# Hybrid decoder step on one core: input projections of both layers by Strassen's seven block products, and four buffers of weight sums in the dense down projection

## What is computed

```python
h = rmsnorm(x, p['norm_mix'][l])                     # (288, 1024)
proj = (h @ p['w_in'][l]).astype(f32)                # its first 3072 columns are retention's q, k, v, g
q, k, v, g = split_cols(p_ret, (512, 512, 1024, 1024))
...
def swiglu(h, w1, w3, w2):                           # layer 0, D_FF = 2816
    return (jax.nn.silu(h @ w1) * (h @ w3)) @ w2
```

## Time and profile before

| what | value |
| --- | --- |
| three runs | 2597.69, 2598.03, 2598.75 us; median 2598.03 |
| the profiled execution | 2598.95 us, of which 2597.1 us are the span from first to last instruction |
| TensorE (PE) busy | 2537.8 us, 98% of the span |
| VectorE (DVE) busy | 984.4 us, 38% |
| ScalarE (ACT) busy | 591.7 us, 23% |
| mean granted TensorE clock | 0.996 |

### The profile page before, as it was taken

How to read it: one execution, slowest core, us unless ns; L and a number is a source line. 1 busy time by engine, 2 the same in 40 slices (tenths; PEclk the granted TensorE clock), 3 DMA queues, 4 the chain that set the end, 5 groups by cost and what they waited for, 6 DMA issues and landing times. The chain is left out here.

```text
span 2597.1 us, 92064 instructions
## 1 busy us (share of the span) xinstructions
PE 2537.8 (98%) x41094; PEld 1990.9 (77%) x41094; DVE 984.4 (38%) x2719; ACT 591.7 (23%) x1773; POOL 0.2 (0%) x4
## 2 busy tenths in 40 slices
PE   8999999999999999999999999999999999999998
PEld 5766666666678999676666666667899999999997
DVE  2022665666515675202267566651311111111111
ACT  2232333333301100123333333330111111111111
POOL 0000000000000000000000000000000000000000
PEclk9999999999999999999999999999999999999999
DMA  6433442222243443333334222234699999999997
GB/s 223 122 121 113 158 153 92 81 77 76 96 143 127 151 155 126 123 114 132 135 127 158 91 84 81 76 104 130 253 371 395 376 368 389 388 370 378 392 370 277
DMA packets 145584, 499.71 MB, mean 192 GB/s; under 512 B 18736, under 2 KB 23472, under 8 KB 142800
## 3 DMA queue, kind: packets, MB, share of 16 engines
q1 hardware_dynamic: 145360, 496.43, 53.6%
HBM read 476.07 MB, written 20.29 MB: 191 GB/s over the span
## 5 line engine op out<-in xcount | busy, mean ns | idle before, releaser
L295 PE MATMUL psum<-hT,ring 128*64 128x288 f32 (+1 forms) x4376 | 540.4, 391 | 1.8 <-DVE hT L2084 1.8
L410 PE MATMUL psum<-work,ring 128*64 128x88 f32 x11264 | 434.7, 239 | 3.5 <-issue 3.5
L410 PEld LDWEIGHTS psum<-work,ring 128*64 128x64 f32 x11264 | 433.2, 136 | 5.9 <-issue 5.7
L295 PEld LDWEIGHTS psum<-hT,ring 128*64 128x64 f32 x4376 | 292.4, 137 | 160.3 <-issue 8.1
L2309 PE MATMUL psum<-work,proj 128*64 128x88 f32 x5632 | 223.7, 239 | 1.0 <-issue 1.0
L2309 PEld LDWEIGHTS psum<-work,proj 128*64 128x64 f32 x5632 | 218.3, 136 | 5.7 <-issue 5.7
L403 PE MATMUL psum<-hT,ring 128*128 128x288 f32 x768 | 187.1, 406 | 0.0
L1461 ACT ACTIVATE work<-psum 128x256 f32<-128x256 f32 (+4 forms) x320 | 104.0, 362 | 349.9 <-PE psum L1374 84.8
L2586 DVE TENSOR_TENSOR work<-psum,work 128x88 f32<-128x88 f32 x176 | 44.2, 251 | 367.6 <-PE psum L410 367.6
L403 PEld LDWEIGHTS psum<-hT,ring 128*128 128x128 f32 x768 | 145.8, 190 | 40.9 <-issue 0.8
L2392 ACT ACTIVATE work<-psum 128x88 f32<-128x88 f32 x176 | 43.1, 245 | 380.5 <-PE psum L410 380.5
(11 more groups left out here) (449 smaller groups left out, 3293.8 us busy)
## 6 DMA issues: line engine op xcount, KB each, us to landing
ring<-w_ff_dram SPq DMA_DIRECT2D x424, 512.0 KB, 6.5
ring<-w_mix_dram SPq DMA_DIRECT2D x256, 512.0 KB, 3.8
proj<-w_ff_dram SPq DMA_DIRECT2D x128, 512.0 KB, 5.4
proj<-w_ff_dram SPq DMA_DIRECT2D x64, 384.0 KB, 5.6
work<-s_gla_dram SPq DMA_DIRECT2D x8, 1024.0 KB, 5.1
gla_s_out<-work SPq DMA_DIRECT2D x8, 1024.0 KB, 4.7
work<-s_ret_dram SPq DMA_DIRECT2D x8, 512.0 KB, 4.7
ret_s_out<-work SPq DMA_DIRECT2D x8, 512.0 KB, 3.1
```

The costliest lines, as they stand in the source:

```text
L295: last = nc.tensor.matmul(out[64 * c:64 * c + 64], weights[:, 64 * c:64 * c + 64], x, start=start, stop=stop)
L410: mm = nc.tensor.matmul(out[64 * c:64 * c + 64], ring[:, s, k, 64 * c:64 * c + 64], rhs[:, k0 + k, :], start=(k0 + k == 0), stop=(k0 + k = ...
```

## The change

It does two things. `project_in` handles its 24 slabs as 12 pairs by the seven block products, with `weight_sums`, `activation_sums`, `combine` and the products moved out of `mix_out` into shared helpers. And the down part of the dense feed-forward uses the same `wsum` memory as four buffers (its sums are at most 128x256), forms sums up to three slabs ahead, waits for them later inside a slab, and puts `combine` and the additions of a group behind the sums of the third slab of the next group.

```diff
+    def seven_products(pe, sig, q, a1, a2, sums, xsums, h, ready=lambda k: None):
+        s1, s2, s3, s4 = sums
+        t1, t2, t3, t4 = (xsums[:, i] for i in range(4))
+        x, y, z = FIRST[q % 2], MIDDLE[q % 2], LAST_TWO[q % 2]   # banks 0,3 / 1,4 / 2,5
+        block_group(x[:, 2 * HALF:3 * HALF], a1[:, 0:4], h[:, 0:4, 0:HALF], ...)
+        block_group(x[:, 0:HALF], a1[:, 4:8], h[:, 4:8, 0:HALF], ...)
+        pe.wait_ge(sig("wsum"), 4 * q + 3)
+        block_group(x[:, HALF:2 * HALF], s2, t2).then_inc(sig("first_ps"), 1)
+        block_group(y[:, 0:HALF], s1, t1)
+        block_group(y[:, HALF:2 * HALF], s3, t3).then_inc(sig("middle_ps"), 1)
+        pe.wait_ge(sig("wsum"), 4 * q + 4)
+        block_group(z[:, 0:HALF], s4, h[:, 4:8, HALF:T])
+        block_group(z[:, HALF:2 * HALF], a2[:, 4:8], t4).then_inc(slab_done, 2)
 # retention, TensorE
-            pe.wait_ge(projected("bank_free"), 3 * RING)
+            pe.wait_ge(projected("evacuated"), 4)
+            pe.wait_ge(projected("taken"), 11)
 # mix_out, TensorE, down part
-                    pe.wait_ge(sig("wsum"), 4 * (FT + n) + 4)
...
+                        if k == 0:
+                            pe.wait_ge(sig("wsum"), 4 * (FT + n) + 3)     # before the third product
...
+                        if k == 0:
+                            pe.wait_ge(sig("wsum"), 4 * (FT + n) + 4)     # before the sixth
 # mix_out, VectorE, down part (sums of slab n in buffer n % 4)
-                dve.wait_ge(slab_done, FF0 + UP_SLABS + (n - 1 if n >= 2 else 2 * n - 2))
+                dve.wait_ge(slab_done, FF0 + UP_SLABS + (n - 3 if n >= 4 else n // 2 * 2 - 2))
...
                     else:
                         down_weight_sums(0)
+                        down_weight_sums(1)
...
-                for n in range(1, DOWN_SLABS + 1):
...
+                for n in range(2, DOWN_SLABS):
+                    down_weight_sums(n)
+                    if n % 6 == 2 and n > 6:
+                        add_pair(n // 6 - 1)          # combine, two add_slab
+                    if n % 6 == 4 and n > 6:
+                        add_squares(n // 6 - 1)
+                add_pair(KT // 2 - 1)
+                add_squares(KT // 2 - 1)
 # project_in, TensorE
-            for n in range(3 * RING):
-                slab_arrived(pe, S_RET, n // RING, n % RING)
-                if n >= 4:
-                    pe.wait_ge(sig("bank_free"), n - 3)
-                slab_products(pe, n % RING, bank[n % 4][:, 0:T], hT)
-                if n == 1:
+            for p in range(PAIRS):                    # 12
+                pair_arrived(pe, p)
+                if p == 1:
+                    pe.wait_ge(sig("z"), 1)
+                if p >= 2:
+                    pe.wait_ge(sig("taken"), p - 1)
+                seven_products(pe, sig, p, ring[...], ring[...], sum_tiles(wsum[:, p % 2], 4, 4), xsum, hT)
+                if p == 0:                            # the four gate products Z, as before
 # project_in, ScalarE
+            def take_first(p):                        # copies one product, 128x144, out of its bank
+            def evacuate(p, func=cp):                 # quad (four quarters, 128x576) -> proj
+                act.wait_ge(sig("taken"), p + 1)
-            evacuate(0)
-            evacuate(1)
+            take_first(0)
             act.wait_ge(sig("z_ps"), 1)
             for h in range(GLA_H):
                 last = ac(z[:, h, :], Z[h][:, 0:T], ...)
             last.then_inc(sig("z"), 1)
+            evacuate(0)
+            take_first(1)
...
 # project_in, VectorE
+            def pair_sums(p):
+                pair_arrived(dve, p)
+                if p >= 2:
+                    dve.wait_ge(slab_done, slabs_before(layer, S_RET) + 2 * p - 2)
+                weight_sums(...)
+            def pair(p):
+                if p >= 2:
+                    dve.wait_ge(sig("evacuated"), p - 1)
+                combine(...)
             # order after the norm: activation_sums, sums 0, mix x2, sums 1, pair 0, sums 2,
             # [wait z, L2753, L2754], pair 1, sums 3, [L2757, L2759], pair 2, sums 4,
             # [scans L2764, in layer 0 the cast L2767], then for p = 3..11: pair p, sums p + 2
```

More of the change, by code:

```diff
@@ L412, in narrow_products, with flat, sum_tiles, block_group @@
         mm.then_inc(slab_done, 1)
+    FIRST, MIDDLE, LAST_TWO = bank[0:6:3], bank[1:6:3], bank[2:6:3]
+    def flat(ap):
+        return ap.rearrange("p n t -> p (n t)")
+    def sum_tiles(region, n, blocks):
+        return (region[:, i, 0:128 * blocks].rearrange("p (k m) -> p k m", m=128) for i in range(n))
+    def block_group(out, weights, x, ready=lambda k: None):
+        for k in range(PAIRS_UP):
+            ready(k)
+            last = in_halves(out, weights[:, k], x[:, k], start=(k == 0), stop=(k == PAIRS_UP - 1))
+        return last
@@ new lines, in combine @@
+    def combine(dve, sig, q, done, c, first):
+        two = lambda b: b[:, 0:2 * HALF].rearrange("p (n t) -> p n t", n=2)
+        dve.wait_ge(sig("first"), q + 1)
+        nc.vector.tensor_tensor(c[:, 0:5:4, :], two(FIRST[q % 2]), rep(first, 1, 2), ALU.add).then_inc(sig("u2"), 1)
+        dve.wait_ge(sig("u2"), q + 1)
+        dve.wait_ge(sig("middle_ps"), q + 1)
+        nc.vector.tensor_tensor(c[:, 5:7, :], two(MIDDLE[q % 2]), rep(c[:, 4, :], 1, 2), ALU.add).then_inc(sig("u34"), 1)
+        dve.wait_ge(sig("u34"), q + 1)
+        dve.wait_ge(slab_done, done)
+        nc.vector.tensor_tensor(c[:, 1:3, :], two(LAST_TWO[q % 2]), c[:, 5:7, :], ALU.add).then_inc(sig("outer"), 1)
+        nc.vector.tensor_tensor(c[:, 3, :], MIDDLE[q % 2][:, 0:HALF], c[:, 6, :], ALU.add).then_inc(sig("taken"), 1)
@@ L1848, in _ @@
         def _(pe):
[L1849 to L1856, removed]
             def logits(k):
@@ L2080, in _, with add_pair, add_squares @@
+            def add_pair(q):
+                c = quad[:, (FT + q) % 2]
+                combine(dve, sig, FT + q, FF0 + UP_SLABS + 6 * q + 6, c, first_product[:, (FT + q) % 2, :])
+                dve.wait_ge(sig("taken"), FT + q + 1)
+                for r in range(2):
+                    add_slab(KT + 2 * q + r, flat(c[:, 2 * r:2 * r + 2, :]))
+            def add_squares(q):
+                for m in range(2 * q, 2 * q + 2):
+                    add_square(KT + m)
             if dense:
@@ L2767, in _ @@
                 nc.vector.tensor_copy(masks[:, :], masks32)
+            for p in range(3, PAIRS):
+                pair(p)
+                if p + 2 < PAIRS:
+                    pair_sums(p + 2)
     for layer in range(DEPTH):
```

168 lines of the change are left out of this document (82 added, 86 removed).

## The result

The changed kernel takes 2579.03 us (median of 4 runs, 2576.24 to 2581.84) against 2598.04 for the kernel before (4 runs, 2597.69 to 2598.75): a ratio of 0.9927, with an interval from 0.9911 to 0.9943. It is faster by 19.0 us, where 26.2 were forecast. Its profiled execution took 2580.26 us, with a span of 2578.4 us and a mean granted clock of 0.995.

The account below looks back on a forecast made before the run. TensorE, busy for 98% of the span, was taken to bound the kernel. Savings of 19.7 us (pairs) and 6.5 us (down part) made 26.2, so 2598.95 became 2572.7 profiled, 2571.8 as median; range 2568.5 to 2578.5.

Parts of the forecast that it names:

- The pairs: Slab stages of both layers: 12 pairs a layer at 6.86 us replace 24 slabs; 19.7 us saved, entries and pause included.
- VectorE's cover: Slab pairs: VectorE's new sums and combines, some 4.3 us per 6.86 us pair, stay hidden with 5.4 us of slack.
- layer 0's pair 3: Tightest place for VectorE: scans and cast come ahead, so its combine starts some 0.5 to 1 us late, still covered.
- The pause at Z: Before pair 1 in each layer: TensorE waits until ScalarE has taken Z out of its banks, 1.92 us.
- The rival: Pause at Z lowers TensorE's clock, costing 3.4 us a layer: 2575.2 us with one layer hit, 2578.6 with both; chance 0.14.
- The entry to retention: After each layer's last pair: 0.2 us of idle time left instead of 0.79, bounds 0 to 0.79.
- I cost all this at nothing: VectorE's new work, first sums, slab loads and refills around the pairs are hidden and add 0 us.
- Part 2: Dense down part: four buffers of weight sums remove all seven gaps, 6.5 us, bounds 0 and 6.6.
- The third rival: Dense down part: the waits only move and the 6.5 us stay, giving 2578.3 us; chance 0.05.
- the fourth: Slab pairs: VectorE comes last, two or three waits of 1 to 3 us give about 2576 us; chance 0.09.
- Loads that don't hide: Slab pairs: records of 144 columns take over 61.25 ns; gain gone from 71 ns, 2630 us at 83 ns; chance 0.02.

Follow-up runs that it names:

- its three variants that keep the idle pause: Changed kernel with 128 semaphore increments, 2586.47 us; with the old down part (pairs alone), 2582.78 us; with 16 short dead products at the start, 2573.72 us.
- the old kernel with the pause: Kernel before, with TensorE made to wait for Z to be taken out before its third slab: 2604.37 us, 1.0023 of the kernel before.
- the pause filled: Changed kernel with 32 extra product records, results never read, between the Z products and the wait for Z: 2571.36 us, 0.9896 of the kernel before.
- Z in two parts: Changed kernel with Z products split behind pairs 0 and 1, in banks 6 and 7, so pair 1 need not wait: 2574.65 us; repeated once, 2574.71 us.

## Why the forecast was right in direction and short in size

**The pairs: right.** 6.86 us a pair, and no wait for `taken`, for a weight sum or for retention's `vst` in either layer. VectorE's cover held everywhere, at the start and at layer 0's pair 3 too. Pair 0, at 7.01, was 0.15 us over. VectorE's busy time grew by 102.6 us where 110 were forecast; by the earlier trace rows a pair's operations add up to 4.2 us, and 4.4 had gone into that sum.

**The pause at Z: right as a wait, short in its consequence.** The step "Now PE stands from 37.73 to 39.51 and a semaphore's way further: 1.92 us" measured 1.86 idle and 4.06 against 4.05 by starts. What failed is the next thought: "Against: pauses of 1.4 us there left the clock at 1.00, and this one has dense work on both sides." Here the clock fell. Of twelve such pauses in six profiled executions (the changed kernel twice, its three variants that keep the idle pause, and the old kernel with the pause), eleven were followed by a lower clock; in ten slab stages without one (the pause filled once, Z in two parts four times) there was none. The length of a pause does not decide it alone: behind the six long waits at the block's end, 2.7 to 2.8 us, the clock fell in four profiles and not in the changed kernel's first nor in the repetition of Z in two parts. The rival had the mechanism with a chance of 0.14, priced by the one fall that the old trace shows, 6.8 us long. Behind this pause the fall is mostly 3.4 us long, so it costs 1.7 us a layer instead of 3.4. Put right, the term is 3.4 us over both layers, and the forecast would have been 2575.2.

**The entry to retention: undersized.** "Between 0 and 0.79, I take 0.2." Some 0.5 was left; PE isn't released at once but stands 0.34 us for VectorE's queue at L274. That is 0.6 us for both layers, inside the bounds given.

**"I cost all this at nothing."** This is the step that took the time out of the range. It named VectorE's work, the loads and the semaphores, and all of those were indeed free as far as the profile shows; the nine semaphores were not measured apart. It left out that 1920 more TensorE records (43014 instead of 41094) are more code, that fetches then fall elsewhere, and that a program already has stalls which depend on it. These cost 1.6 us behind layer 1's recurrent part and 3.1 us in the experts, far from any line that was changed. Nothing in the trace of before says whether this term would be +5 or 0. But its list of waits has 3.5, 2.6 and 1.0 us in exactly these three rows, so such stalls were there and a few microseconds in size, and they deserved a bound on either side. The changed kernel's repetition, 2579.82 us, lies outside the range for the same reason.

**Part 2: right.** 75.7 us against 75.8 forecast, all seven gaps gone, and nothing moved behind them. The third rival fell, and the fourth, with VectorE last in the pairs, showed nowhere.

**Loads that don't hide: the rival did not come.** 61.25 ns a record of 144 columns, with loads of 64, held in the new place. By the Trainium skill, TensorE: Matmul & The Clock Gate, section Back-to-back issue gap, it would have been about 81 ns at 128 columns; the trace has a shorter spacing for more columns here too.

Together: 26.2, less 3.4 for the clock, 0.6 at the entries, 4.7 for the stalls, some 0.7 at pair 0 and the start, and with 1.7 of luck before the dense part, is 18.5 of the 18.7 us between the profiled executions.

## What to carry to other kernels

When an edit brings a new idle stretch on TensorE into dense work, price it twice: the pause, and the lower granted clock behind it, 1.7 us for a pause of 1.86 us here. Either give PE something harmless to do or reorder so that the pause vanishes; the second gave 6.5 us in the profile, the first 3.3. This long straight program has stalls that move when code is added far from them: leave some 5 us of its 2580 for them when you forecast, compare an edit's stages instead of its total when you judge it, and try a few dead instructions in an idle place before you believe that a small gain or loss belongs to the edit.

## What was not expected of the hardware

- A pause of 1.86 us between dense stretches was followed by 3.4 us (once 6.8) at 1.2 GHz in 11 of 12 cases; pauses of 1.4 us in the old down part were not the earlier trace rows, and waits of 2.7 to 2.8 us at the block's end were in four of six.
- The clock before the dense up part fell for 3.4 us in one profile of the changed kernel and for 6.8 in the other, and for nothing and 6.8 us in the two of Z in two parts. From the start of the first dense group to that of the next it is 4.59 us with a fall of 3.4 us as with none, so only the longer fall costs, some 1.7 us that come and go without any edit.
- The start of the first slab product scatters by 2 us (26.16 to 28.14) in kernels with the same work ahead of it, with the moment at which the clock first stays at 2.4 GHz.
- 128 semaphore increments in a row held TensorE back for some 12 us beyond an idle stretch of 10.
- A 117 KB store that took 2.8 to 3.1 us to land (20 times) took 4.6 us with one 16 KB instruction fetch beside it (6 times out of 6).
